# Hybrid mLSTM/short-conv and grouped mixture-of-experts layer: where zero rows are stored, where late stores are awaited, and the order of the last expert's work

## The reference

```python
probs = softmax(xf @ router_w + router_b)                   # 16 experts in 4 groups
grp = argmax(top_k(pg, 2)[0].sum(-1))                       # one group per token
top_p, top_local = top_k(in_grp, 2)                         # its two best experts
gates = top_p / top_p.sum(-1, keepdims=True)
hdn = silu(xb @ w_gate[e]) * (xb @ w_up[e]);  y = hdn @ w_down[e]
y_token = sum over its two experts of gate * y
x = layer_norm(ALPHA * x + y_token, ln_moe_g, ln_moe_b)
```

## Time and profile before

| what | value |
|---|---|
| median of 3 runs | 1715.93 us (1715.03 to 1716.71) |
| profiled execution, its own time | 1715.41 us |
| its span, first to last instruction | 1713.2 us |
| mean granted TensorE clock in it | 0.973 of full speed |
| PE, weight load, DVE, ACT, POOL busy | 94%, 82%, 63%, 38%, 20% of the span |
| DMA | 279.46 MB, mean 163 GB/s |
| mixer; route; experts, about | 0 to 950; 950 to 978; 978 to 1713 us |

### The profile page before, as it was taken

One profiled execution on the slowest core, in us unless ns is written; L12 is line 12 of the kernel. 1 busy time (PEld: TensorE's weight loads), 2 busy tenths in 40 slices (PEclk: granted clock), 3 DMA queues, 4 the chain that ended last, 5 costly groups with the idle time before them and its releaser, 6 DMA issues. The chain is left out here.

```text
span 1713.2 us, 25162 instructions
## 1 busy us (share of the span) xinstructions
PE 1615.4 (94%) x9494; PEld 1398.8 (82%) x9494; DVE 1086.8 (63%) x1799; ACT 659.3 (38%) x919; POOL 340.6 (20%) x271
## 2 busy tenths in 40 slices
PE   6999999999999999999999289999999999999993
PEld 4888888888888888888887178999999999999982
DVE  3436867557676468665586756555676667666676
ACT  2324424143332343342432324344555445544540
POOL 1100005100052001250000012222332323232332
PEclk8999999999999999999999679999999999999997
DMA  7332245332434225352223626666777777777761
GB/s 232 127 99 74 100 146 198 99 98 87 160 139 158 74 75 186 108 182 92 80 93 123 258 84 200 190 203 204 235 250 249 228 238 251 252 228 239 249 182 56
DMA packets 118922, 279.46 MB, mean 163 GB/s; under 512 B 14689, under 2 KB 16865, under 8 KB 118289
## 3 DMA queue, kind: packets, MB, share of 16 engines
q1 hardware_dynamic: 92112, 190.78, 32.8%
q0 software_dynamic: 26112, 84.95, 16.8%
q10 hardware_dynamic: 576, 2.10, 0.3%
HBM read 232.80 MB, written 48.40 MB: 164 GB/s over the span
## 5 line engine op out<-in xcount | busy, mean ns | idle before, releaser
L1054 PE MATMUL mix_acc<-mix_xT_high,mix_w_high 128*128 128x512 f32 x640 | 256.4, 401 | 7.5 <-DVE mix_w_low L791 7.5
L791 DVE TENSOR_TENSOR mix_w_low<-mix_w_raw,mix_w_high 128x2048 fp32r<-128x2048 f32 x73 | 168.5, 2309 | 144.7 <-ACT mix_w_high L646 144.4
L1056 PE MATMUL mix_acc<-mix_xT_high,mix_w_low 128*128 128x512 f32 x640 | 250.9, 392 | 0.0
L1055 PE MATMUL mix_acc<-mix_xT_low,mix_w_high 128*128 128x512 f32 x640 | 250.1, 391 | 0.0
L646 ACT ACTIVATE mix_w_high<-mix_w_raw 128x2048 fp32r<-128x2048 f32 x73 | 139.8, 1915 | 243.4 <-PE mix_acc L1056 224.2
L1789 DVE TENSOR_TENSOR moe_gate_up_low<-kept_w_gate_up_raw,moe_gate_up_high 128x2048 fp32r<-128x2048 f32 x64 | 146.6, 2291 | 80.3 <-ACT moe_gate_up_high L1661 80.3
L2117 PE MATMUL moe_gate_psum<-moe_xT_high,moe_gate_up_high 128*128 128x288 f32 x512 | 154.2, 301 | 1.4 <-DVE moe_xT_low L1806 1.4
L2119 PE MATMUL moe_up_psum<-moe_xT_high,moe_gate_up_low 128*128 128x288 f32 x512 | 152.1, 297 | 0.0
L2118 PE MATMUL moe_gate_psum<-moe_xT_low,moe_gate_up_high 128*128 128x288 f32 x512 | 151.9, 297 | 0.0
L2118 PE MATMUL moe_up_psum<-moe_xT_low,moe_gate_up_high 128*128 128x288 f32 x512 | 151.8, 296 | 0.0
L2117 PE MATMUL moe_up_psum<-moe_xT_high,moe_gate_up_high 128*128 128x288 f32 x512 | 151.6, 296 | 0.0
(11 more groups left out here) (441 smaller groups left out, 3493.2 us busy)
## 6 DMA issues: line engine op xcount, KB each, us to landing
mix_w_raw<-in_w_in SPq DMA_DIRECT2D x57, 1024.0 KB, 5.3
kept_w_gate_up_raw<-in_w_gate SPq DMA_DIRECT2D x32, 1024.0 KB
kept_w_gate_up_raw<-in_w_up SPq DMA_DIRECT2D x32, 1024.0 KB
kept_w_down_raw<-in_w_down SPq DMA_DIRECT2D x32, 1024.0 KB, 10.1
mix_w_raw<-in_w_out SPq DMA_DIRECT2D x16, 1024.0 KB, 5.0
mix_x_rows<-in_x POOLq DMA_DIRECT2D x16, 512.0 KB, 4.5
kept_conv_or_residual<-in_x POOLq DMA_DIRECT2D x16, 512.0 KB, 5.8
x<-kept_conv_or_residual POOLq DMA_DIRECT2D x12, 512.0 KB, 3.3
```

Source lines behind the costliest of these rows:

```text
L791: dve.tensor_tensor(wl[:, stage % 2], raw[:, stage % 2], wh[:, stage % 2].bitcast(F32), ALU.subtract).then_inc(split_l, 1)
L1054: pe.matmul(out, ah, bh, start=first, stop=False)
L1055: pe.matmul(out, ah, bl, start=False, stop=False)
L1056: return pe.matmul(out, al, bh, start=False, stop=last)
```

## The change

It has five parts.

1. The four stores of zeros are issued by POOL right after it has cleared the tile; SP no longer issues them nor waits for them before its loop; its wait stands at stage 5, ahead of the load that overwrites the tile.
2. In `route` neither SP nor ACT waits for its last stores. The semaphores are kept, and `experts` waits for them: POOL and DVE ahead of their loops, ACT ahead of its first `moe_down_high`. The tile that ACT stores from (`alpha_x1`) lies at other addresses, behind a placeholder, clear of what `experts` writes first. No line of the change touches the router's weights.
3. `list_one_hots` is cut into three parts, at experts 0, 1 and 2; PE's product and `lists` move from expert 1 to expert 3.
4. The tail: PE does A, U, the first half of B, the small matmul, the second half of B; B's halves go to two other banks (`gate_psum0`, `up_psum0`), so B waits no more for the sum of A. DVE's order is A, U, first half of B, mean of U, second half of B, norms of U, B, A, and the three list tiles last. The first of the two list tiles of expert 14 is normed at the start of expert 15.
5. POOL's last stores: the three out-of-bounds ones come first, then U, B, A, and the three list tiles last.

```diff
@@ mixer, SP @@
-            sp.wait_ge(stay_made, 1)
-            for k in range(4):
-                sp.dma_start(acc_dram[S + k * P:S + (k + 1) * P], XN[:, 0]).then_inc(zero_out, 16)
-            sp.wait_ge(zero_out, 4 * 16)
             with sp.Fori(0, NG) as g:
                 for stage in range(1, ST):
                     load_stage(g, stage, 0)
...
                     if stage == 5:
+                        sp.wait_ge(zero_out, 4 * 16)
+                        sp.sem_inc(sp_idle, 1)
@@ mixer, POOL @@
             pool.memset(XN[:, 0], 0.0).then_inc(stay_made, 1)
+            pool.wait_ge(stay_made, 1)
+            for k in range(4):
+                pool.dma_start(acc_dram[S + k * P:S + (k + 1) * P], XN[:, 0]).then_inc(zero_out, 16)
@@ route @@
-        AX = sb("alpha_x1", [P, RT, D])
...
+        sb("gate_up_to_come", [P, (2 * 3 * 2 * KC - RT * KC) * P - BANK])
+        AX = sb("alpha_x1", [P, RT, D])
...
-            sp.wait_ge(x1_out, RT * 16)
...
-            act.wait_ge(ax_out, RT * 16)
@@ experts, POOL, ahead of its loop @@
+            for stored_late in (keep.late_x1, keep.late_acc):
+                wait_apart(pool, idle, stored_late, RT * 16)
@@ experts, POOL, the tail @@
                 list_store(r, LAST - 1)
-                list_store(r, LAST)
...
-                for n, (k, to, most, index) in enumerate(((U, ...), (A, ...), (B, ...))):
-                    wait_apart(pool, idle, end_normed, r * COLS + n + 1)
-                    end_store(r, n, k, to, most, END_OUT[k], index, end_stored)
+                wait_apart(pool, idle, end_var, r * COLS + COLS)
                 for k, to, most in ((U, quarter_rows, ...), (A, acc_dram, ...), (B, acc_dram, ...)):
-                    end_store(r, n, k, to, most, END_IN[k], back_i[:, k:k + 1], end_stored)
+                    end_store(to, most, END_IN[k], back_i[:, k:k + 1])
+                for n, (k, to, most, index) in enumerate(((U, ...), (B, ...), (A, ...))):
+                    wait_apart(pool, idle, end_normed, r * COLS + n + 1)
+                    end_store(to, most, END_OUT[k], index)
+                list_store(r, LAST)
@@ experts, ACT @@
             def split_dn(r, e):
+                if e == 0:
+                    act.wait_ge(keep.late_acc, RT * 16)
...
-                for n, k in enumerate((U, A, B)):
+                for n, k in enumerate((A, U, B)):
                     end_rstd_of(r, n, k)
@@ experts, DVE @@
+            dve.wait_ge(keep.late_x1, RT * 16)
             with dve.Fori(0, n_rounds) as r:
...
+                    if e == LAST:
+                        row_norm(r, LAST - 1, 0, 1)
                     hidden(r, e, 0)
...
-                    if e == 1:
+                    if e == 3:
                         lists(r)
...
-                    if e == 0:
-                        list_one_hots(r)
-                    row_norm(r, e - 1)
+                    if e < 3:
+                        list_one_hots(r, e)
+                    row_norm(r, e - 1, 1 if e == LAST else 0)
...
                 row_stats(r, LAST)
+                end_sums(r, A)
                 end_sums(r, U)
+                dve.wait_ge(end_half, r + 1)
+                dve.wait_ge(end_in[B], r * 16 + 16)
+                end_add(r, B, 0)
                 end_quarters(r)
-                end_norm(r, 0, U)
-                end_sums(r, A)
+                end_sums(r, B)
+                end_norm(r, 1, U)
+                end_norm(r, 2, B)
+                end_norm(r, 0, A)
                 row_norm(r, LAST)
-                end_norm(r, 1, A)
-                end_sums(r, B)
-                end_norm(r, 2, B)
@@ experts, PE @@
+            def down_end(r, q):
+                s = slice(q * BANK, (q + 1) * BANK)
+                for c in range(FC):
+                    ins = three(end_ps[q][:], hTh[:, c, AT[B]], hTl[:, c, AT[B]], dh[:, c, s], dl[:, c, s],
+                                c == 0, c == FC - 1)
+                ins.then_inc((end_half, b_used)[q], 1)
...
-                        pe.wait_ge(end_sum, r * COLS + 2)
...
+                        down(r, e, A)
                         down_last(r, e)
-                        down(r, e, A)
+                        pe.wait_ge(hid_done, r * (NE * FC) + NE * FC - 1)
+                        down_end(r, 0)
                         pe.wait_ge(end_sq_done, r + 1)
                         pe.matmul(px[0][:, 0:2], same[:], end_sq[:], start=True, stop=True).then_inc(end_mean, 1)
-                        down(r, e, B)
+                        down_end(r, 1)
```

More of the change, by code:

```diff
@@ L1906, in backs, with list_one_hots @@
                 dve.tensor_scalar(same[:], px[1][:, 0:P], 1.0 / QUARTERS, None, ALU.mult).then_inc(same_done, 1)
-            def list_one_hots(r):
+            def list_one_hots(r, part):
                 def do(instruction):
@@ L1922, in list_one_hots @@
                 in_last = of_group[:, :, GROUPS - 1]
+                if part == 2:
+                    own.step(dve.tensor_tensor(LISTLO, keep.i128[:].unsqueeze(1).to_broadcast([P, TILES, P]),
+                                               low_f.unsqueeze(2).to_broadcast([P, TILES, P]), ALU.is_equal))
+                    do(dve.tensor_tensor(LISTCOL, keep.icol[:, 0:NLIST].unsqueeze(1).to_broadcast([P, TILES, NLIST]),
+                                         at.unsqueeze(2).to_broadcast([P, TILES, NLIST]), ALU.is_equal))
+                    do(dve.tensor_tensor(LISTCOL, LISTCOL, keep.tokp1[:].unsqueeze(2).to_broadcast([P, TILES, NLIST]),
+                                         ALU.mult))
+                    dve.sem_inc(list_oh, 1)
+                    return
+                if part == 1:
+                    own.step(dve.tensor_tensor(ok, at, most, ALU.is_lt))
+                    own.step(dve.tensor_scalar(kept_at, at, 0.0, None, ALU.is_ge))
+                    own.step(dve.tensor_copy(at_i, at))
+                    own.wait(r)
+                    own.step(dve.tensor_tensor(ok, ok, kept_at, ALU.mult))
+                    own.step(dve.tensor_scalar(low_i, at_i, P - 1, None, ALU.bitwise_and))
+                    own.step(dve.tensor_scalar(at_i, at_i, 7, None, ALU.arith_shift_right))
+                    own.wait(r)
+                    own.step(dve.tensor_copy(low_f, low_i))
+                    own.step(dve.tensor_copy(at, at_i))
+                    for g in range(GROUPS):
+                        ins = dve.tensor_scalar(per_group[:, :, g], of_group[:, :, g], float(LIST_AT[g]), None, ALU.mult)
+                    own.step(ins)
+                    own.wait(r)
+                    do(dve.tensor_reduce(most, per_group, AX_.X, ALU.add))
+                    do(dve.scalar_tensor_tensor(out=at, in0=at, scalar=1.0, in1=most, op0=ALU.add, op1=ALU.add))
+                    do(dve.tensor_tensor(at, at, ok, ALU.mult))
+                    do(dve.tensor_scalar(at, at, -1.0, None, ALU.add))
+                    return
                 do(dve.tensor_reduce(sums.rearrange("p t g -> p (t g)"),
@@ L1994, in row_stats, with row_norm @@
                 ins.then_inc(var_done, 1)
-            def row_norm(r, e):
+            def row_norm(r, e, first=0, end=RTILES):
                 if e not in BATCH:
@@ L2001, in row_norm @@
                 dve.wait_ge(rs_done, r * len(BATCHES) + BATCHES.index(e) + 1)
-                for n, i in enumerate(BATCH[e]):
+                for n, i in list(enumerate(BATCH[e]))[first:end]:
                     rows = R[row_tile(i)]
@@ L2128, in turn_x @@
                     pe.wait_ge(same_done, r + 1)
-                if k == A and e == 2:
+                if k == A and e == 4:
                     pe.wait_ge(lists_done, r + 1)
```

91 lines of the change are left out of this document (35 added, 56 removed).

## The result

Four executions of the changed kernel took 1697.80 to 1701.43 us, median 1698.69; four of the kernel before, 1715.03 to 1717.19, median 1716.32. The ratio is 0.9899, 95% interval 0.9883 to 0.9915: 17.6 us faster by the medians. The forecast was 1696.5, range 1693.5 to 1704.5. In the profiled execution (1698.55 us) the span is 1696.2 us against 1713.2, the granted clock 0.977 against 0.973.

What follows compares the result with a forecast made beforehand. PE was taken as full in the mixer and mid-experts, so only its idle places could give time: start -9.2, route -1.4, expert 0 -1.4, tail -7.4, sum -19.4, from 1715.4 to 1696.0, plus 0.5 for the median: 1696.5 us, range 1693.5 to 1704.5.

Steps and rivals of the forecast that it cites:

- The start, -9.2: At the kernel's start: PE's 7.5 us wait for stage 1 and the slow clock behind it go; 9.2 us saved.
- Two of my own signs of being wrong: Listed for the changed profile: PE still waiting over 2 us for stage 1, and a fall of the clock behind it.
- First rival: Start: the zero rows come fully ahead of the first weights; start -5.0 in place of -9.2, 1700.7 us; 15%.
- Second rival: Start: constants land so late beside the zeros that stage 1's wait stays whole; start 0, 1705.7 us; 6%.
- Route, -1.4: End of route: the engines' meeting, reading the number of rounds and loop entry behind SP's wait go; 1.4 us saved.
- Expert 0, -1.4: Expert 0: list tables cut in three let `hidden` start on time, so PE's 1.41 us wait goes; 1.4 us saved.
- List product, 0: Experts: the list product and its clock fall move from expert 1 to expert 3 unchanged; 0 us.
- Tail, -7.4: Tail: DVE ends 4.7 us earlier, POOL 8.4, the end behind POOL grows 1.0; 7.4 us saved.
- Third rival: Tail: the second half of B runs at half clock after PE's pause, costing 2.6 us more; 1699.1 us; 8%.
- Fourth rival: Route to experts: DVE's wait for late row stores makes it slower than before, about 1721.5 us if 25 late; 3%.
- the terms at their small bounds: Whole kernel: every term at its smallest expected gain, together -10.7 us, giving 1705.2 us.

Runs made afterwards that it cites:

- start_undone: The changed kernel with the zero stores back in SP's queue and SP waiting for them before it loads stage 1; 1704.63 us, ratio 0.994.
- stage1_first: The changed kernel with stage 1's load issued right behind stage 0's, ahead of all constants; 1702.21 us, ratio 0.9921.
- changed_again: The changed kernel run once more, nothing altered; 1699.65 us, ratio 0.9912.
- tables_one_run: The changed kernel with the three parts of the list tables made in one run in expert 0 again; 1703.70 us, ratio 0.9932.

## Why the prediction was right, and where it was not

- **The start, -9.2: the term that was mis-sized.** Measured -4.9 in the first profile and -3.7 in the median of eight. The wait of 7.5 and the half clock behind it were read rightly, and both go when nothing stands in the way (9.5 and 9.7). The step that failed is the price of the zeros: "from 12 to 17 us the DMA engines are half idle (share 0.52 in the row at 14), which swallows some 2.5 of the 5.3 us. I take 0.5 us lost". The engines were half idle while tiny pieces went through them; time so lost isn't room for another queue. I priced only the bytes, not that SP itself issues later: stage 1 left at 21.2 to 23.7, not 18.8. The 7.8 us that I gave it to land (5.3 and 2.5) were about right. In the first profile the zeros cost 4.8 us of the full 9.7: some 3.3 by the later issue, the rest, by my estimate, by the clock that fell again (3.4 us at half pace lose 1.7). Two of my own signs of being wrong came: a wait of over 2 us, and a fall of the clock behind it.
- **First rival, start -5.0, 1700.7.** It had 15%. Its size came out, its mechanism didn't. Stage 0's low part was begun 1.0 us later than before, but that isn't the zeros' doing: it is begun at 14.8 to 16.1 us in the eight profiles with early zeros and at 15.0 to 16.0 in the five without (the kernel before, `start_undone` and the three with the zeros late). ACT didn't wait for stage 0's weights in any of these thirteen. The loss was in SP's issue of stage 1. (Its sum has a slip as well: 36.3 less 33.7 is a wait of 2.6, not 2.1, so the bound is -4.5.) The Trainium skill, DMA: Bandwidth & Descriptors, section Queues, rings and completion order, has the engines go round the queues packet by packet; the slower issue on SP beside the zeros (3.48 against 1.60 us) is in keeping with it, but the delay of stage 0 that I drew from it didn't come.
- **Second rival, constants late.** In `stage1_first` it came true (5.5 us of wait, last constant at 32.18). In the eight profiles with the changed start it didn't: ACT's wait before stage 1 is ended by the weights each time, not by a constant. What the constants' loads did there was to leave SP's queue late, and stage 1 behind them.
- **Route, -1.4.** Measured -1.4, and +1.0 to 1.5 when the waits are put back. DVE's wait stayed, ended by a DMA, as forecast.
- **Expert 0, -1.4.** Measured -1.7 and 1.8: PE's wait of 1.41 and a little more, within the bounds.
- **List product, 0.** Right on average; the gain of 1.4 in the first pair of traces was the clock's, by chance.
- **Tail, -7.4.** Measured -7.6. DVE's end 4.0 nearer (forecast 4.7; the wait at the second half of B was 1.36, not 1.1, and the first statistics began 0.2 later than said), POOL's end 7.8 nearer (8.4), and the end behind it 0.2 longer, not 1.0. The errors cancel. The order of POOL's stores alone is 3.9, the early norm 2.0 by its mark (1.2 by the medians, 3.3 in the profile in which the clock fell too). PE's own new order (A ahead of U, halves of B) wasn't tried alone. The estimate of 1.2 us for the bytes of a last store, worked out from the figures of the Trainium skill, DMA: Bandwidth & Descriptors, section Anatomy of one DMA, is not borne out: the end came 5.5 us behind the full store and 5.3 to 5.4 behind an empty one.
- **Third rival, the second half of B at half clock.** It didn't come at 1.4 us; at 2.5 us it did, for 1.5 us more and not 2.6.
- **Fourth rival, slower by DVE's wait.** It was 2.58 us, as short as forecast, and can be removed.

That 1698.7 came so near 1696.5 owes something to chance: the start gave 4.3 less, and the list product 1.4, expert 0 0.3 and the tail 0.2 more. The profile was a lucky one, too: the stretch to the first sigmoid was the shortest of thirteen (median 38.6). The same kernel's second median, 1699.65, is 3.2 above the forecast. And the range isn't what it is said to be: it ends at 1704.5, while the terms at their small bounds give 1705.2.

## What to carry to other kernels

A DMA share of 0.4 at a few GB/s was not idle capacity here: loads of tiny pieces were going through, and 2.1 MB in a second queue beside them made the queue that issues them 2.4 to 4.9 us late. Put bulk transfers that nobody needs soon behind a wait for the first thing that somebody does need. When one queue is relieved by moving work to another, list everything that is in flight at the new moment; and profile the same kernel twice before a difference of one or two us between two traces is explained.

## What the runs showed of the hardware

- The granted clock behind a pause of PE is not the same from run to run. At stage 1 it stayed at 1.00 behind pauses of 0.5, 0.6 and 1.4 us; behind 2.2 to 5.5 us (seven profiles) it went to 0.50 for 3.4 us, behind 7.5 (the kernel before) for 6.8 and behind 6.6 (`start_undone`) for 10.2 (the low stretches, read from the table by 2 us). The length of the pause alone doesn't set how long it stays down.
- The clock column can miss a fall: in `changed_again` it says 1.00 from 16 to 20 us, while the products start 0.43 us apart, the pace of 0.50 in the other profiles. At the places above, the count of products per window agrees with the column.
- Behind the 32 small products of the lists it stayed up in eight of thirteen profiles (the expert 3.5 to 3.6 us longer than the steady 41.68), and fell for 3.4 us in four (5.1 to 5.2 longer) and 6.8 in one (6.7 longer).
- The 64 slot products of the first tables took 9.1 to 10.7 us in the thirteen profiles. They start at 0.50; in the first profile the clock was back 3.7 us later, in `tables_one_run` after 7.
- A store all of whose rows are out of bounds takes POOL 1.29 us like a full one, and the program ends 5.4 us behind it, as behind a full one (5.5).
